# The last token tile of a mixer-and-experts step: router on blocks of x ahead of LayerNorm

## The reference

```
mix = _mixer(x, ...)                        # combined projection, GLA and pooling branches, gates, w_out
h   = LayerNorm(alpha * x + mix, ln1_g, ln1_b)
logits = h @ w_router + b_router            # 32 columns
top_v, top_i = top_k(logits, 4); gate_w = softmax(top_v)
f   = sum over the 4 experts of gate_w * (swiglu(h @ w_gu[e] + b_gu[e]) @ w_down[e] + b_down[e])
y   = LayerNorm(alpha * h + f, ln2_g, ln2_b)
```

## Time and profile before

| what | value |
|---|---|
| median of the timed runs | 1268.34 us (3 runs, 1265.9 to 1268.51) |
| the profiled execution, its own time | 1269.73 us |
| its span in the trace | 1268.0 us |
| TensorE busy | 1162.3 us, 92% of the span |
| VectorE busy | 467.2 us, 37% |
| ScalarE busy | 248.4 us, 20% |
| GpSimd busy | 27.5 us, 2% |
| DMA | 454.50 MB, mean 358 GB/s |
| mean granted TensorE clock | 0.991 of full |

### The profile page before, as it was taken

One profiled execution on the slowest core, in us unless ns is written; L12 is line 12 of the kernel. 1 busy time (PEld: TensorE's weight loads), 2 busy tenths in 40 slices (PEclk: granted clock), 3 DMA queues, 4 the chain that ended last, 5 costly groups with the idle time before them and its releaser, 6 DMA issues.

```text
span 1268.0 us, 15570 instructions
## 1 busy us (share of the span) xinstructions
PE 1162.3 (92%) x6265; PEld 640.4 (50%) x6265; DVE 467.2 (37%) x796; ACT 248.4 (20%) x407; POOL 27.5 (2%) x44
## 2 busy tenths in 40 slices
PE   6999999999999999998898899989898988898884
PEld 6999999998543433433343234334333423343331
DVE  4575666665533232322222231223222222322135
ACT  4544344420211111111111111111111101110112
POOL 0000100100000000000000000000000000000001
PEclk9999999999899999999999999999999999999997
DMA  9526444692499999999999999999999999999993
GB/s 380 204 101 241 137 170 158 230 365 83 167 428 423 428 427 427 426 428 427 428 428 428 427 428 428 428 427 428 429 427 427 428 429 427 427 428 428 427 424 132
DMA packets 37945, 454.50 MB, mean 358 GB/s; under 512 B 4461, under 2 KB 4589, under 8 KB 9096
## 3 DMA queue, kind: packets, MB, share of 16 engines
q1 hardware_dynamic: 33744, 439.62, 83.0%
q0 software_dynamic: 4160, 14.29, 3.3%
HBM read 447.70 MB, written 6.31 MB: 358 GB/s over the span
## 4 chain that ended last, share of the span: by engine, by line
DMA 51%; PE 44%; DVE 3%; ACT 1%; issue 1%; SPq 0%; DVEq 0%; ACTq 0%
DMA ring<-in_w_gu 31%; DMA ring<-in_w_down 19%; PE bank L1009 13%; PE bank L706 12%; PE bank L1037 6%; PE bank L774 3%; PE bank L749 2%; PE bank L1061 1%; PE bank L982 1%; PE bank L833 1%; PE bank L820 1%; DMA ring<-in_w_mix 1%; PE bank L761 1%; DVE arena L1626 1%; PE bank L823 1%
## 5 line engine op out<-in xcount | busy, mean ns | idle before, releaser
L1009 PE MATMUL bank<-ring,arena 128*64 128x512 f32 x1504 | 339.8, 599 | 44.0 <-DMA ring<-in_w_gu 44.0
L1009 PEld LDWEIGHTS bank<-ring,arena 128*64 128x64 f32 x1504 | 103.7, 137 | 258.7 <-issue 182.8
L1037 PE MATMUL bank<-ring,arena 128*64 128x512 f32 x784 | 178.7, 598 | 18.0 <-DMA ring<-in_w_down 17.7
L706 PE MATMUL bank<-arena_r,ring_r 128*128 128x320 f32 x848 | 182.3, 316 | 0.0
L1865 DVE SCALAR_TENSOR_TENSOR arena_r<-bank,arena,arena_r 64x512 fp32r<-64x512 f32 x62 | 46.4, 749 | 289.5 <-ACT arena_r L1408 289.0
L706 PEld LDWEIGHTS bank<-arena_r,ring_r 128*128 128x128 f32 x848 | 138.7, 188 | 0.6 <-issue 0.4
L1828 DVE COPY arena<-bank 128x512 f32<-128x512 f32 x32 | 22.1, 692 | 290.6 <-PE bank L1009 290.6
L1009 PE MATMUL bank<-arena 128*64 128x512 f32 x528 | 119.8, 596 | 7.7 <-DMA arena<-in_w_gu 7.4
L1037 PEld LDWEIGHTS bank<-ring,arena 128*64 128x64 f32 x784 | 54.1, 136 | 121.9 <-issue 99.3
L1396 ACT ACTIVATE arena<-bank 128x512 f32<-128x512 f32 x32 | 19.1, 598 | 423.4 <-PE bank L1009 423.4
L1499 DVE TENSOR_TENSOR ring_r<-ring,ring_r 128x1024 fp32r<-128x1024 f32 x56 | 67.8, 1224 | 56.5 <-ACT ring_r L1225 56.3
(11 more groups left out here) (258 smaller groups left out, 957.8 us busy)
## 6 DMA issues: line engine op xcount, KB each, us to landing
ring<-in_w_gu SPq DMA_DIRECT2D x94, 2048.0 KB, 35.0
ring<-in_w_down SPq DMA_DIRECT2D x48, 2048.0 KB, 35.1
arena<-in_w_gu SPq DMA_DIRECT2D x33, 2048.0 KB, 35.2
ring<-in_w_mix SPq DMA_DIRECT2D x32, 1024.0 KB, 5.2
arena<-in_w_down SPq DMA_DIRECT2D x15, 2048.0 KB, 35.1
arena<-in_state_gla POOLq DMA_DIRECT2D x4, 1024.0 KB, 6.8
out<-arena POOLq DMA_DIRECT2D x4, 1024.0 KB, 5.6
alone<-in_w_gu SPq DMA_DIRECT2D x1, 2048.0 KB, 9.3
```

Source lines behind the costliest of these rows:

```text
L706: last = mm(o[:, 0:NT], w[a][:, c, f0:f0 + 128], rhs[b][:, c, :], start=c == 0 and a + b == 0, stop=c == chunks - 1 and a == 1)
L1009: last = mm(ex[i][side * CAP:(side + 1) * CAP, :], xgt[:, 2 * j + c, block * CAP:(block + 1) * CAP], w[:, c, i * D + side * 512:i * D + (s ...
L1037: last = mm(out[side * CAP:(side + 1) * CAP, :], actt[:, 4 * j + c, :], w[:, c, side * 512:(side + 1) * 512], start=j == 0 and c == 0, sto ...
```

## The change

- **Router of tile 1.** Tile 1 no longer waits for its LayerNorm: the four blocks of x (256 columns each) are transposed as they come out of the output projection (`turn_block`, two transposes each, products `xb` 0 to 3), ACT copies them, and `router_block` multiplies them by `wr_gain`, the router's weights times the gain of LayerNorm. `route` then applies mean and scale with two instructions in place of one.
- **The fold.** DVE forms `wr_gain` and `wr_bias` (weights times bias) and sums both over its eight chunks (four new instructions ahead of the pooling windows); PE sums them over the partitions with one matmul against ones, the new product `fold`, ahead of `gb` 0; DVE turns the result into `wr_rows` (two new instructions behind `low_after` of `gb` 5) and frees the bank.
- **LayerNorm of tile 1.** DVE does the lower 512 columns. For the upper 512 ACT subtracts the mean and scales, GpSimd multiplies by the gain and adds the bias.
- **Gather of tile 1.** It reads h of tile 1 in float32 with a float32 one-hot (`last_gather`), with no wait for the split in two parts; that split moves behind, to where the second gather needs it. The count of tokens per expert (`count_tokens`) moves between the first two units of expert 0. Of the four places with `keep_clock` matmuls two stay: 12 matmuls before, 4 now.

The core of the diff (register and semaphore declarations cut):

```diff
-            + [("pb",), ("up",), ("us",)] + [("gb", i) for i in range(6)] + [("grp", i) for i in range(4)]
+            + [("pb",), ("up",), ("us",), ("fold",)] + [("gb", i) for i in range(6)] + [("grp", i) for i in range(4)]
...
-            + [("lg", 0), ("out", 2, 1), ("rk", 0), ("out", 3, 1), ("ht", 1, 0), ("ht", 1, 1), ("lg", 1)]
+            + [("lg", 0), ("xb", 0), ("out", 2, 1), ("rk", 0), ("xb", 1), ("out", 3, 1), ("xb", 2), ("lg", 1), ("xb", 3)]
...
+        wr_gain = reg(FOLD, 256, KC)
+        wr_bias = reg(QE, 256, KC)
+        wr_sums = reg(FOLD + 256, 2 * NE, 2)
+        wr_rows = reg(FOLD + 320, 2 * NE, 2)
+        shift1 = reg(FOLD + 384, 1)
+        oh1 = reg(OH1, 128)
...
+            upper = hrow[:, 1, 512:]
+            pool.wait_ge(ln1_in, 32)
+            pool.wait_ge(white1, 1)
+            nc.gpsimd.tensor_tensor(upper, upper, ln1[0][:, 512:], ALU.mult).then_inc(gain1, 1)
+            pool.wait_ge(gain1, 1)
+            nc.gpsimd.tensor_tensor(upper, upper, ln1[1][:, 512:], ALU.add).then_inc(h1_ready, 1)
...
+            pe.wait_ge(fold_ready, 1)
+            o = claim(("fold",))
+            mm(o[:, 0:2 * NE], cst("ones"), wr_sums.rearrange("p a e -> p (a e)"), start=True, stop=True)\
+                .then_inc(full(("fold",))[0], 1)
...
+            def turn_block(j):
+                pe.wait_ge(freed(("out", j, 1)), NO[("out", j, 1)] // 8 + 1)
+                o = claim(("xb", j))
+                for c in range(2):
+                    f0 = j * 256 + c * 128
+                    last = nc.tensor.transpose(o[:, c * 128:(c + 1) * 128], xr[:, 1, f0:f0 + 128], ident)
+                last.then_inc(full(("xb", j))[0], 1)
+            def router_block(j):
+                pe.wait_ge(xb_ready, j + 1)
+                for c in range(2 * j, 2 * j + 2):
+                    last = mm(bank(("lg", 1))[:, 0:NE], ot[:, c, 128:256], wr_gain[:, c, :], start=c == 0, stop=c == KC - 1)
+                return last
...
+            def last_gather(half):
+                for c in range(4 * half, 4 * half + 4):
+                    last = mm(ex[6 + half][:, (c % 4) * 128:(c % 4 + 1) * 128], hrow[:, 1, c * 128:(c + 1) * 128], oh1,
+                              start=False, stop=True, skip_group_check=True)
+                last.then_inc(gathered, 1)
...
             router(0, 4)
+            turn_block(0)
             tokens_times("out", 2, 1, ga)
             ranks(0, 3)
+            turn_block(1)
             tokens_times("out", 3, 1, ga)
+            turn_block(2)
+            claim(("lg", 1))
+            router_block(0)
+            router_block(1)
+            turn_block(3)
+            router_block(2)
+            router_block(3).then_inc(full(("lg", 1))[0], 1)
             released(6)
-            released(7)
             pe.wait_ge(rows_zero, 1)
             pe.wait_ge(onehot_early, 1)
             pe.wait_ge(parts_ready, 2)
-            for half in range(2):
-                first_gather(ORDER[:2], half, True)
+            first_gather(ORDER[:2], 0)
+            ranks(1, 4)
+            released(7)
+            first_gather(ORDER[:2], 1)
             spare = claim(("gwt",))
             keep_clock(2)
-            turn_h(1, 5)
-            keep_clock(2)
-            router(1, 6)
-            keep_clock(6)
-            ranks(1, 4)
-            o = claim(("cnt",))
-            for t, (t0, n) in enumerate(TILES):
-                last = mm(o[0:1, 0:NE], cst("ones", p=n, n=1), msk[0:n, t, :], start=t == 0, stop=t == 2)
-            last.then_inc(full(("cnt",))[0], 1)
-            keep_clock(2)
+            def count_tokens():
...
-            pe.wait_ge(onehot_ready, 1)
-            pe.wait_ge(parts_ready, 3)
-            for half in range(2):
-                first_gather(ORDER[2:], half, False).then_inc(gathered, 1)
+            pe.wait_ge(oh1_ready, 1)
+            pe.wait_ge(h_ready, 5)
+            last_gather(0)
+            pe.wait_ge(h1_ready, 1)
+            last_gather(1)
+            keep_clock(2)
             released(0)
             released(1)
-            expert_up(units(True, 0), 0, gathers=1)
+            expert_up(units(True, 0), 0, gathers=1, between=[count_tokens], after=(0,))
...
-            for i, t in enumerate(ORDER):
+            for i, t in enumerate(ORDER[:2]):
                 n = TILES[t][1]
                 act.wait_ge(var_ready, i + 1)
                 A(rstd[0:n], mv[0:n, 1:2], ACT.Sqrt, bias=eps_ln[0:n]).then_inc(std_ready, 1)
...
                 act.wait_ge(ht_ready, 2 * i + 2)
                 for half in range(2):
                     act.sem_inc(freed(("ht", t, half)), 1)
+            for j in range(4):
+                if j == 3:
+                    act.wait_ge(var_ready, 3)
+                    A(rstd, mv[:, 1:2], ACT.Sqrt, bias=eps_ln).then_inc(std_ready, 1)
+                act.wait_ge(*full(("xb", j)))
+                A(ot[:, 2 * j:2 * j + 2, 128:256], bank(("xb", j))[:, 0:256].rearrange("p (c n) -> p c n", n=128), ACT.Copy)\
+                    .then_inc(xb_ready, 1)
+                act.wait_ge(xb_ready, j + 1)
+                act.sem_inc(freed(("xb", j)), 1)
+            act.wait_ge(shift1_ready, 1)
+            A(hrow[:, 1, 512:], xr[:, 1, 512:], ACT.Identity, scale=rstd, bias=shift1).then_inc(white1, 1)
...
+            dve.wait_ge(late_in, 48)
+            V.tensor_tensor(wr_gain, wrt, cols[:, 26:34].unsqueeze(2).broadcast_to([128, KC, NE]), ALU.mult)
+            link(V.tensor_tensor(wr_bias, wrt, cols[:, 34:42].unsqueeze(2).broadcast_to([128, KC, NE]), ALU.mult))
+            V.tensor_reduce(wr_sums[:, 0, :], wr_gain.rearrange("p c e -> p e c"), mybir.AxisListType.X, ALU.add)
+            V.tensor_reduce(wr_sums[:, 1, :], wr_bias.rearrange("p c e -> p e c"), mybir.AxisListType.X, ALU.add)\
+                .then_inc(fold_ready, 1)
...
+            dve.wait_ge(*full(("fold",)))
+            V.tensor_scalar(wr_rows[:, 0, :], bank(("fold",))[:, 0:NE], -1.0, None, ALU.mult)
+            V.tensor_tensor(wr_rows[:, 1, :], bank(("fold",))[:, NE:2 * NE], brt, ALU.add).then_inc(fold_done, 1)
+            dve.wait_ge(fold_done, 1)
+            dve.sem_inc(freed(("fold",)), 1)
...
+                if t == 1:
+                    link(V.scalar_tensor_tensor(lg[:, 1, :], wr_rows[:, 0, :], mv[:, 0:1], bank(("lg", 1))[:, 0:NE],
+                                                ALU.mult, ALU.add))
+                    link(V.scalar_tensor_tensor(lg[:, 1, :], lg[:, 1, :], rstd, wr_rows[:, 1, :], ALU.mult, ALU.add))
...
-                link(centred(xr[:, t, :], hrow[:, t, :], 128, t + 2, ln1[0], rstd))
-                scaled(hrow[:, t, :], 128, rstd, ln1[1], h_ready)
-                split_h(t + 1, t)
+                if t == 0:
+                    link(centred(xr[:, t, :], hrow[:, t, :], 128, t + 2, ln1[0], rstd))
+                    scaled(hrow[:, t, :], 128, rstd, ln1[1], h_ready)
+                    split_h(t + 1, t)
+            lower_half = hrow[:, 1, 0:512]
+            dve.wait_ge(ln_step, normed[0])
+            V.bn_aggr(mv, st6).then_inc(var_ready, 1)
+            dve.wait_ge(var_ready, 3)
+            link(V.scalar_tensor_tensor(lower_half, xr[:, 1, 0:512], mv[:, 0:1], ln1[0][:, 0:512], ALU.subtract, ALU.mult))
+            dve.wait_ge(std_ready, 3)
+            link(V.reciprocal(rstd, rstd))
+            V.scalar_tensor_tensor(shift1, mv[:, 0:1], -1.0, rstd, ALU.mult, ALU.mult).then_inc(shift1_ready, 1)
             route(2, 1)
-            first_onehot(1).then_inc(onehot_ready, 1)
+            V.scalar_tensor_tensor(lower_half, lower_half, rstd, ln1[1][:, 0:512], ALU.mult, ALU.add).then_inc(h_ready, 1)
+            dve.wait_ge(*full(("rk", 1)))
+            V.tensor_tensor(rank[:, 1, 0:NE], bank(("rk", 1))[:, 0:NE], msk[:, 1, :], ALU.mult).then_inc(freed(("rk", 1)), 1)
+            dve.wait_ge(freed(("rk", 1)), NO[("rk", 1)] // 8 + 1)
+            for e in range(2):
+                last = V.tensor_scalar(oh1[:, e * CAP:(e + 1) * CAP], cst("iota64"), rank[:, 1, e:e + 1], None, ALU.is_equal)
+            last.then_inc(oh1_ready, 1)
+            for e in range(2):
+                last = V.tensor_scalar(onehot[:, 0, 1, e * CAP:(e + 1) * CAP], cst("iota64"), rank[:, 1, e:e + 1], None,
+                                       ALU.is_equal)
+            last.then_inc(onehot_ready, 1)
...
+            dve.wait_ge(h1_ready, 1)
+            split_h(2, 1)
```

More of the change, by code:

```diff
@@ L144 @@
 WRT = GA2 + 640
+OH1 = WRT + 256
+FOLD = BB + 1088
 SP = 17408
@@ L152 @@
 COLS = BGU + 512
-BR = COLS + 32
+BR = COLS + 42
 PACKED = BR + NE - CONST
@@ L156 @@
 MISC = DEC + 48
-ARENA = MISC + 64
+ARENA = MISC + 48
 EARLY = 1
@@ L289, in build @@
         bgu = reg(BGU, 512, 16)
-        cols = reg(COLS, 26)
+        cols = reg(COLS, 42)
         dec = reg(DEC, 48, HEADS)
@@ L421, in build @@
         onehot_ready = sem("onehot_ready")
+        fold_ready = sem("fold_ready")
+        fold_done = sem("fold_done")
+        xb_ready = sem("xb_ready")
+        shift1_ready = sem("shift1_ready")
```

(36 more changed lines are left out.)

12 lines of the change are left out of this document (8 added, 4 removed).

## The result

| | before | changed |
|---|---|---|
| median of the timed runs | 1267.12 us (4 runs, 1265.33 to 1268.51) | 1280.22 us (4 runs, 1279.81 to 1281.24) |
| profiled execution, own time | 1269.73 us | 1280.13 us |
| span | 1268.0 us | 1278.2 us |
| first slot of the ring given back | 340.57 us | 350.63 us |
| mean granted TensorE clock | 0.991 | 0.989 |

The changed kernel is slower: ratio 1.0105, 95% interval 1.0088 to 1.0123, which is 13.3 us by the ratio. The direction was forecast; the size was not (+7.3 us, 1275.6 us, range to 1280.0 us; the median lies just outside it). One run of the kernel before, timed beside e1 to e4, took 1321.71 us at a granted clock of 0.846, and the ratios leave it out.

The account below looks back on a forecast made before the run. PE's chain was taken to bound the kernel up to the first slot, the DMA stream after it. Waits +7.8, clock in them +3.3, start of the experts -3.8 gave +7.3 us, 1275.6 us on the median; range 1270.3 to 1280 us.

Parts of the forecast that it names:

- first wait: Ahead of `gb` 0: PE rests until DVE's sums for the fold are ready, +3.9 us (3.3 to 4.6).
- second wait: Between the first and second group product: PE rests until DVE frees the fold's bank 2, +3.9 us (3.5 to 4.3).
- clock in the waits: Behind PE's two rests at the fold: one fall to half clock each, 1.65 us apiece, +3.3 us.
- output blocks: End of tile 1's output projection: two block transposes ahead of the last blocks delay the last one by 0.5 us.
- last block of x to expert 0: From tile 1's last output block to expert 0: about 10.7 us instead of 14.5 us.
- expert 0 to the first slot: First units of expert 0: the moved token count adds 0.4 us; a partly regained clock takes off 0.8 us.
- What bounds the kernel: PE's chain bounds the part before the first slot returns; the DMA stream behind it is unchanged, so the end moves equally.
- the start of the experts: Tile 1's router, top 4 and gather up to the first units: shorter by 3.0 us, taken as -3.8 us with the clock.
- The clock in the new order: Ahead of expert 0: gain 5.6 us if the clock stays up, 3.0 us if it falls; -3.8 us taken.
- GpSimd beside DVE: Two GpSimd instructions beside DVE's top 4 of tile 1: contention of 0 to 1 us, taken as 0.
- the change doesn't bring its own gain: Rival: GpSimd takes twice its time, the upper half of h is late, expert 0 no sooner; +11.5 us, 1279.8 us; chance 0.07.
- The other edits: ACT's and GpSimd's parts beside PE and the later split of tile 1, hidden in expert 0: cost nothing.

Follow-up runs that it names:

- e1: Changed kernel with the fold's matmul moved behind `gb` 7 and its two DVE instructions behind the low parts of `gb` 7; 1269.03 us, ratio 1.0015 to the kernel before.
- e4: Changed kernel with 24 matmuls of 320 columns, results unread, ahead of the fold's matmul; 1278.61 us, ratio 1.0093 to the kernel before.
- e8: The kernel before, unchanged, run once more for another profile; 1265.76 us in one run.
- e2: Changed kernel with only the fold's matmul moved, behind `gb` 0, its DVE instructions left in place; 1273.47 us, ratio 1.0046 to the kernel before.
- e3: Changed kernel with only the two DVE instructions on the fold moved, behind the low parts of `gb` 1; 1276.48 us, ratio 1.0066 to the kernel before.
- e6: e1 plus seven `keep_clock` matmuls of 512 columns: two ahead of the last router block, five behind the gather's first half; 1264.77 us, ratio 0.9991 to the kernel before.
- e5: e1 with GpSimd's two instructions on the upper half of h held until DVE's top 4 of tile 1 is done; 1267.48 us, ratio 1.0012 to the kernel before.
- e7: e1 with tile 1's upper half of h made by DVE alone, plus four `keep_clock` matmuls; 1263.58 us, ratio 0.9979 to the kernel before.

## Why the prediction was wrong, step by step

The sum of what was measured, against a run of before with the clock up (e8), goes from the start of the last transposes of the pooling inputs to the first slot: 350.63 - 229.67 us after, 336.64 - 229.24 us before, which is 13.6 us more. The parts (the forecast is the prediction's, against its own base, the first profile of before):

| step | forecast | measured | from |
|---|---|---|---|
| first wait, with the matmul of the fold | +3.9 | +4.3 | `gb` 0 at 234.59 after transposes at 229.67 us; 229.84 after 229.24 us |
| second wait | +3.9 | +3.8 | 3.83 us of rest |
| clock in the waits | +3.3 | +4.1 | 23.41 and 21.97 us for 21.13 and 21.14 us; group products 1.0 us |
| output blocks (two block transposes) | +0.5 | +0.3 | 286.96 to 328.62 us after; 274.27 to 315.59 us in e8 |
| last block of x to expert 0 | -3.9 | +0.4 | 14.38 and 13.94 us |
| expert 0 to the first slot (forecast: count +0.4, clock -0.8) | -0.4 | +0.5 | 7.63 and 7.11 us |
| sum (measured: of the two differences above; the rounded parts give 13.4) | +7.3 | +13.6 | |

- **What bounds the kernel.** Right: the first slot moved by 10.1 us from profile to profile and the span by 10.2 us. In all ten profiles the time from the first slot to the end is the same within 1 us, 927.2 to 928.2 us.
- **The two waits.** Right in place, cause and size; e2 and e3 take away one each, e1 both. The first cost 0.4 us more than was counted, because the fold's own matmul, counted at 0.2 us, took 0.69 us with the clock down behind the rest (0.43 us with the clock up, in e2 and e4).
- **The clock in the waits.** Right, one fall in each; a size was off by 0.8 us, because the first fall lasted 6.8 us. e4 shows the first of them by itself.
- **The step that failed is "the start of the experts".** It was priced at -3.8 us. Against e8 it brought +1.3 us. Against the profile that it was read from, it brought -2.0 us; there the whole came to +10.3 us, and of the 3.0 us above the forecast 1.8 lie in this step and 1.2 in the waits. Three terms of the step were mis-sized.
  - The base. The half clock of 6.8 us was read as a property of the kernel before; e8 is a run without it, and the median of 26 runs lies near e8. Of the first profile's time it is 3.2 us. Against a run without it the instructions alone promised 3.0 us and not 5.6 us, and a fall in the new order eats that.
  - The clock in the new order. 0.8 us were counted as regained. The clock falls at 334.96 us, and nothing is regained: against the rows with the clock up, the second half of the gather costs 1.7 us more (3.65 and 1.98 us), the two `keep_clock` matmuls 0.5 us (1.16 and 0.68 us), the gather of tile 1 1.0 us (2.98 and 1.95 us), 3.2 us in all. e6, which differs from e1 by seven matmuls that fill PE's rests, is 3.0 us faster.
  - GpSimd beside DVE was set to 0 us. It held DVE for 1.5 us, of which 0.9 us lay ahead of the mask; e5 gives 0.8 us of that back in the profile. The earlier trace rows had a sign of it that was not put into the sum: two DVE instructions took 2.77 us beside GpSimd. (The pair it was compared with was no clean measure, since it reads PSUM and had GpSimd beside its end, from 1257.06 us; two of the same line with 64 partitions and no GpSimd took 1.42 us, at 1262.90 us.)
  
  Together, with the 3.0 us that the instructions promised: -3.0 + 3.2 + 0.9 = +1.1 us, of the +1.3 us measured against e8.
- **The rival "the change doesn't bring its own gain"** (0.07, 1279.8 us) came nearest to the time, but not by the mechanism that it named: GpSimd's result was there at 334.94 us and PE read it behind 339.62 us, so the upper half was never late.
- **The range** ended at 1280.0 us, at that rival's 1279.8 us, with no room for the base of the profiled run or for the first fall's length.
- **The other edits** cost nothing that shows, except the token count between the first units: 0.35 us in the chain.

What stays open: why the clock falls ahead of expert 0 in one profile of the kernel before and not in the other. The rows show that both happen, with the same instructions. Two profiles cannot say how often.

## What to carry to other kernels

Precomputing weights is work that PE runs in its program order: put its matmul where its input has been ready for long, and its PSUM bank where nobody comes back to it before the taker is due; here the place in PE's and DVE's order was worth 11.4 us. When a stretch before a bound stream is made shorter, read the granted clock of it in more than one profile of the old kernel, since a fall in the one at hand may be luck. A helper engine beside a chain of short instructions can hold the chain until its own instruction ends: have it start behind the chain, or leave the work where it was.

## What the runs showed of the hardware

- A short DVE instruction that copies, or that has one input and a scalar, ended only when a GpSimd instruction of 128x512 that was under way had ended: 1.05 us for a copy of 128x8 (0.17 us alone) and 0.83 us for 128x4 (0.22 us), both ending within 0.03 us of GpSimd's. The reduction beside it (L1822, 0.38 us) and, in e5, the product that reads PSUM (L1906, 0.19 us) kept their times. The Trainium skill, "GPSIMD Engine Reference" (Key points), names contention with DVE instructions in a 2-port mode or with two SBUF inputs. The second kind agrees with e5, where GpSimd took 1.74 us behind the DVE instruction L1904 with two SBUF inputs. Whether the copy and the 128x4 instruction ran in a 2-port mode no trace shows; what the traces show is that the price is the rest of the other engine's instruction, not a lower pace.
- The clock fell with PE busy for most of the time before: in the changed kernel PE had rested for 0.44 and 1.16 us and run matmuls of 32 and 128 columns. With seven matmuls of 512 columns in the rests it stayed at 2.4 GHz (e6), with four as well (e7).
- The float32 gather of 128 columns costs what the fp32r gather costs per matmul: 16 in 1.95 us and 16 in 1.98 us (both e6).
